# The input projection of the matrix memory in seven quarter products per weight tile

## The reference, cut to what matters

```python
MLSTM_INNER = 2 * D_MODEL       # 2048
def mlstm_mixer(u, w_in, conv_w, conv_b, wq, wk, wv, w_gates, b_gates, norm_w, skip, w_out):
    xm, z = jnp.split(u @ w_in, 2, axis=-1)
    xc = jax.nn.silu(causal_depthwise_conv(xm, conv_w, conv_b))
    q = block_diag_proj(xc, wq)
    k = block_diag_proj(xc, wk)
    v = block_diag_proj(xm, wv)
    ...
    h = (h * norm_w + skip * xc) * jax.nn.silu(z)
    return h @ w_out
```

## Time and profile before

| | us |
|---|---|
| median of three runs | 2719.5 (2718.7 to 2721.1) |
| profiled execution, its own time | 2724.7 |
| its span in the trace | 2722.9 |
| TensorE busy | 2636.3 |
| VectorE / ScalarE / GpSimd busy | 791.6 / 402.8 / 755.3 |

### The profile page before, as it was taken

The page is one execution under the profiler, slowest core; times in us unless marked ns, Lnnn a source line. Parts: engine busy times, 40 slices in busy tenths (PEclk is TensorE's granted clock), DMA queues, the critical chain, the costliest instruction groups (busy, mean ns, idle before and its releaser), DMA issues.

```text
span 2722.9 us, 44432 instructions
## 1 busy us (share of the span) xinstructions
PE 2636.3 (97%) x19521; PEld 1838.0 (68%) x19521; DVE 791.6 (29%) x1463; ACT 402.8 (15%) x813; POOL 755.3 (28%) x585
## 2 busy tenths in 40 slices
PE   7999999989999999999999999999999999999998
PEld 5767888856644444444445436488888878998998
DVE  3316310064300001100013494232221136532651
ACT  0032010020211001000002244110000121221000
POOL 0042055074000000000000260145555331622886
PEclk8999999999999999999999999999999999999999
DMA  9878544468499999999997210332222243122542
GB/s 304 305 256 280 143 158 155 144 250 290 170 353 408 407 373 379 396 390 407 376 387 271 81 47 8 105 105 78 93 85 86 78 139 108 49 76 93 171 162 87
DMA packets 318290, 561.70 MB, mean 206 GB/s; under 512 B 45544, under 2 KB 181520, under 8 KB 317968
## 3 DMA queue, kind: packets, MB, share of 16 engines
q1 hardware_dynamic: 299280, 554.57, 57.2%
q10 hardware_dynamic: 18816, 4.27, 0.8%
HBM read 557.75 MB, written 1.05 MB: 205 GB/s over the span
## 4 chain that ended last, share of the span: by engine, by line
PE 56%; issue 34%; POOL 3%; DVE 2%; POOLq 2%; ACT 1%; DMA 1%; DVEq 1%; SPq 0%; ACTq 0%
PE psum L984 13%; PE psum L1829 10%; PE psum L2058 5%; PE psum L1866 5%; PE psum L1912 3%; PE psum L1150 3%; PE psum L2086 2%; PE psum L1305 2%; PE psum L1932 2%; PE psum L1645 2%; PE psum L1025 1%; PE psum L1959 1%; POOLq L3685 1%; DMA ring<-in_ada_w 1%; POOLq L3583 1%
## 5 line engine op out<-in xcount | busy, mean ns | idle before, releaser
L1507 PE MATMUL psum<-ring,xe 128*32 128x512 f32 (+1 forms) x4608 | 458.0, 557 | 1.6 <-issue 1.4
L1507 PEld LDWEIGHTS psum<-ring,xe 128*32 128x32 f32 x4608 | 152.5, 110 | 294.7 <-issue 255.2
L984 PE MATMUL psum<-act_in,ring 128*128 128x256 f32 x1216 | 269.7, 382 | 2.4 <-DVE act_in L2671 1.3
L984 PEld LDWEIGHTS psum<-act_in,ring 128*128 128x128 f32 x1216 | 231.2, 191 | 42.7 <-issue 9.3
L3684 POOL TENSOR_TENSOR ckv<-ckv,nstat 128x512 f32<-128x512 f32 x2 | 2.5, 1276 | 894.8 <-DVE nstat L3229 894.8
L1529 PE MATMUL psum<-ring,zs 128*32 128x256 f32 x4224 | 232.4, 379 | 0.8 <-DMA ring<-in_moe_w 0.8
L3120 DVE TENSOR_TENSOR act_in<-act_in,psum 128x256 f32<-128x256 f32 (+1 forms) x72 | 28.7, 399 | 630.8 <-ACT act_in L2368 630.8
L1529 PEld LDWEIGHTS psum<-ring,zs 128*32 128x32 f32 x4224 | 137.8, 110 | 97.7 <-issue 7.1
L3697 POOL TENSOR_TENSOR w_sums<-ring 128x512 f32<-128x512 f32 (+1 forms) x34 | 42.3, 1243 | 298.0 <-DVE ctxT L3286 123.8
L2368 ACT ACTIVATE act_in<-psum 128x256 f32<-128x256 f32 (+1 forms) x72 | 26.4, 367 | 573.4 <-PE psum L1507 573.4
L1645 PE MATMUL psum<-a,ring 128*128 128x512 f32 x224 | 97.5, 594 | 2.0 <-ACT a L2417 1.3
(11 more groups left out here) (551 smaller groups left out, 4204.2 us busy)
## 6 DMA issues: line engine op xcount, KB each, us to landing
ring<-in_moe_w SPq DMA_DIRECT2D x216, 1024.0 KB, 11.2
ring<-in_ffn_w SPq DMA_DIRECT2D x97, 1024.0 KB, 5.2
ring<-in_ada_w SPq DMA_DIRECT2D x96, 1024.0 KB, 7.9
ring<-in_moe_w SPq DMA_DIRECT2D x64, 768.0 KB, 6.1
ring<-in_hg_w_in SPq DMA_DIRECT2D x20, 1024.0 KB, 5.1
ring<-in_mlstm_w_in SPq DMA_DIRECT2D x16, 1024.0 KB, 6.2
ring<-in_mlstm_w_out SPq DMA_DIRECT2D x8, 1024.0 KB, 7.4
ring<-in_s_w_glu SPq DMA_DIRECT2D x8, 1024.0 KB, 11.6
```

The costliest lines, as they stand in the source:

```text
L984: last = pe.matmul(bank(j)[:, n * T:(n + 1) * T], tile[:, k * width + n * P:k * width + (n + 1) * P], src(k), start=start and k == 0, stop ...
L1507: last = pe.matmul(psum[rows, r, 0:2 * nb * 32].rearrange("p (u b f) -> p u b f", u=2, b=nb), xe[:, k, at:at + 32], tile[:, :, :, rows], s ...
```

## The change

Each input tile is now computed by one step of Winograd's form of Strassen's method. The 1024 inputs, the 256 outputs of a tile and the 256 tokens are each cut in half. The plain method then is eight products of 512 inputs, 128 outputs and 128 tokens; here there are seven, and additions:

- GpSimd forms four sums of quarters of each weight tile, 128 x 512 each, into `in_w_sums` (two sets, by the parity of the tile). Sum set i waits for the tile's landing and for the last product of tile i - 2. `xT` times the constant moves behind the sums of tile 6, and the work behind the stage waits for the last join, since the buffers lie in `qk`.
- VectorE forms three sums of the activations once (`in_x_sums`, and one in place in `act_in`), between the modulation and the first join.
- TensorE makes seven products (`input_tile`), in the order 1, 2, 6, 5, 7, 3, 4. Product 6 is the first that needs a weight sum (and, for tile 0, the activations' sums). A tile now takes two jobs, the first with products 1, 2 and 6. Of each modulation step the two halves stay behind the tile, but `gate_weights` now stands between the halves.
- ScalarE only copies product 1 out of PSUM (`in_first`); VectorE joins (`join`): five additions, each with one input in PSUM and one in SBUF. The SiLU of `zs` is done in place after the join, one tile later.
- VectorE convolves between the joins, one block per tile up to tile 4, then three per tile, until the 16 blocks are done after tile 8. Gate fold and block diagonals come after joins 9, 10 and 11. ScalarE does the convolution's SiLUs under tiles 8 to 15.

Elsewhere only semaphore counts shift by 16, 8 or 4.

```diff
+INPUT_TILES = 16
...
-JOBS = [("params", 1), ("xT", 4), ("late_params", 4), ("m_in", 8 + EARLY_Z), ("m_fold", 4), ("m_z", 8 - EARLY_Z), ("m_qk", 16), ("m_fsel", 1),
+JOBS = [("params", 1), ("xT", 4), ("late_params", 4), ("m_in", 2 * (8 + EARLY_Z)), ("m_fold", 4), ("m_z", 2 * (8 - EARLY_Z)), ("m_qk", 16), ("m_fsel", 1),
...
+        in_flat = qk.rearrange("p c k t -> p (c k t)")
+        in_w_sums = in_flat[:, 1024:5120].rearrange("p (n i k s) -> p n i k s", n=2, i=4, s=P)
+        in_x_sums = in_flat[:, 5120:6656].rearrange("p (i k t) -> p i k t", i=3, t=P)
+        in_first = in_flat[:, 6656:6912].rearrange("p (n t) -> p n t", n=2)
+        in_with_sixth = in_flat[:, 6912:7040]
+        in_with_two = in_flat[:, 7040:7296].rearrange("p (m t) -> p m t", m=2)
...
+        def in_quarters(i):
+            v = ring[:, in_tile(i) % RING].rearrange("p (e k f s) -> p e k f s", e=2, k=4, f=2)
+            return {(f, e): v[:, e, :, f] for f in range(2) for e in range(2)}
+        def in_product(i, m, n=1):
+            b, at = SMALL_AT[m]
+            return bank(in_job(i) + b)[:, at * P:(at + n) * P]
...
+                def input_tile(i):
+                    wait_tile(pe, in_tile(i))
+                    quarter, sums = in_quarters(i), in_w_sums[:, i % 2]
+                    operands = {1: (quarter[0, 0], lambda k: act_in[:, k, 0:P]),
+                                2: (quarter[0, 1], lambda k: act_in[:, 4 + k, 0:P]),
+                                6: (sums[:, 1], lambda k: in_x_sums[:, 1, k]),
+                                5: (sums[:, 0], lambda k: in_x_sums[:, 0, k]),
+                                7: (sums[:, 2], lambda k: act_in[:, k, P:T]),
+                                3: (sums[:, 3], lambda k: act_in[:, 4 + k, P:T]),
+                                4: (quarter[1, 1], lambda k: in_x_sums[:, 2, k])}
+                    for m, (held, moving) in operands.items():
+                        if m in (1, 5):
+                            wait_free(pe, in_job(i) + SMALL_AT[m][0])
+                        if m == 6:
+                            pe.wait_ge(S("w_sums_ready"), i + 1)
+                        if i == 0 and m in (6, 7, 4):
+                            pe.wait_ge(S("x_sums_ready"), {6: 2, 7: 3, 4: 4}[m])
+                        for k in range(4):
+                            if i == 0 and m in (1, 2):
+                                pe.wait_ge(S("mlstm_in_ready"), (0 if m == 1 else 4) + k + 1)
+                            last = pe.matmul(in_product(i, m), held[:, k], moving(k), start=k == 0, stop=k == 3)
+                            if m == 1 and k == 0:
+                                last.then_inc(tile_begun, 1)
+                        if m in (6, 4):
+                            full(last, in_job(i) + SMALL_AT[m][0])
...
-                    mm_pair(in_tile(j), in_job(j), lambda k: act_in[:, k],
-                            before=(lambda k: pe.wait_ge(S("mlstm_in_ready"), k + 1)) if j == 0 else None)
-                    if FIRST_INPUT - 1 <= j < FIRST_INPUT - 1 + UNDER_INPUT:
-                        ada_step("b", j - FIRST_INPUT + 1, 1)
+                    input_tile(j)
+                    under = FIRST_INPUT - 1 <= j < FIRST_INPUT - 1 + UNDER_INPUT
+                    if under:
+                        ada_half("b", j - FIRST_INPUT + 1, 1, 0)
                     if j == 7 + EARLY_Z:
                         gate_weights()
+                    if under:
+                        ada_half("b", j - FIRST_INPUT + 1, 1, 1)
...
+                def z_silu(i):
+                    wait_out(act, in_job(i) + 1)
+                    act.activation(zs[:, 2 * i - 16:2 * i - 14], zs[:, 2 * i - 16:2 * i - 14], ACT.Silu).then_inc(S("gate_silu_ready"), 1)
                 for i in range(16):
-                    j = in_job(i)
-                    wait_full(act, j)
-                    src = bank(j).rearrange("p (a t) -> p a t", a=2)
-                    if i < 8:
-                        out_of(act.activation(xm[:, 2 * i:2 * i + 2, 4:4 + T], src, ACT.Copy), j)
-                    else:
-                        out_of(act.activation(zs[:, 2 * i - 16:2 * i - 14], src, ACT.Silu), j)
+                    if i >= 2:
+                        wait_out(act, in_job(i - 2) + 1)
+                    wait_full(act, in_job(i))
+                    act.activation(in_first[:, i % 2], in_product(i, 1), ACT.Copy).then_inc(S("first_out"), 1)
+                    if i >= 9:
+                        z_silu(i - 1)
+                    if i >= 8:
+                        for c in (2 * i - 16, 2 * i - 15):
+                            act.wait_ge(S("conv_sum_ready"), c + 1)
+                            act.activation(xc[:, c], xc[:, c], ACT.Silu, bias=col("mlstm_conv_b", c)).then_inc(S("conv_ready"), 1)
+                z_silu(15)
...
-                    act.wait_ge(S("conv_sum_ready"), c + 1)
-                    act.activation(xc[:, c], xc[:, c], ACT.Silu, bias=col("mlstm_conv_b", c)).then_inc(S("conv_ready"), 1)
-                    if c >= 2:
-                        j = job_of["m_qk"] + c - 2
-                        wait_full(act, j)
-                        out_of(act.activation(qk[:, c - 2, 0], bank(j)[:, 0:T], ACT.Copy), j)
-                for c in range(IC - 2, IC):
...
+                x11, x12, x21, x22 = act_in[:, 0:4, 0:P], act_in[:, 0:4, P:T], act_in[:, 4:8, 0:P], act_in[:, 4:8, P:T]
+                dve.drain()
+                dve.tensor_tensor(in_x_sums[:, 0], x12, x11, ALU.subtract).then_inc(S("x_sums_ready"), 1)
+                dve.drain()
+                dve.tensor_tensor(in_x_sums[:, 1], x22, in_x_sums[:, 0], ALU.subtract).then_inc(S("x_sums_ready"), 1)
+                dve.tensor_tensor(x12, x22, x12, ALU.subtract).then_inc(S("x_sums_ready"), 1)
+                dve.drain()
+                dve.tensor_tensor(in_x_sums[:, 2], x21, in_x_sums[:, 1], ALU.subtract).then_inc(S("x_sums_ready"), 1)
+                def join(i):
+                    if i < 8:
+                        flat = xm.rearrange("p c t -> p (c t)")[:, 2 * i * (T + 4):(2 * i + 2) * (T + 4)]
+                        first_at, last_at = flat[:, 4:4 + P], flat[:, T + 8 + P:2 * (T + 4)]
+                        between = flat[:, 4 + P:4 + P + 2 * (P + 4)].rearrange("p (m t) -> p m t", m=2)[:, :, 0:P]
+                    else:
+                        flat = zs[:, 2 * i - 16:2 * i - 14].rearrange("p c t -> p (c t)")
+                        first_at, last_at = flat[:, 0:P], flat[:, 3 * P:4 * P]
+                        between = flat[:, P:3 * P].rearrange("p (m t) -> p m t", m=2)
+                    dve.wait_ge(S("first_out"), i + 1)
+                    dve.tensor_tensor(first_at, in_first[:, i % 2], in_product(i, 2), ALU.add)
+                    out_of(dve.tensor_tensor(in_with_sixth, in_first[:, i % 2], in_product(i, 6), ALU.add), in_job(i))
+                    dve.drain()
+                    wait_full(dve, in_job(i) + 1)
+                    dve.tensor_tensor(in_with_two, in_with_sixth[:, None, :].broadcast_to([P, 2, P]),
+                                      in_product(i, 5, 2).rearrange("p (m t) -> p m t", t=P), ALU.add)
+                    dve.drain()
+                    dve.tensor_tensor(last_at, in_with_two[:, 1], in_product(i, 5), ALU.add)
+                    out_of(dve.tensor_tensor(between, in_with_two, in_product(i, 3, 2).rearrange("p (m t) -> p m t", t=P),
+                                             ALU.add), in_job(i) + 1)
+                    dve.drain()
+                def convolve(c):
...
+                done = 0
+                for i in range(16):
+                    join(i)
+                    for c in range(done, min(done + (1 if i < 5 else 3), IC)):
+                        convolve(c)
+                        done = c + 1
+                    if i == 7 + EARLY_Z:
+                        fold_gates()
+                    elif i == 8 + EARLY_Z:
+                        query_key_rows()
+                        block_diagonals(0, qk_small)
+                    elif i == 9 + EARLY_Z:
+                        block_diagonals(2, qkv_small[:, 2])
...
-            pool.wait_ge(S("mlstm_in_ready"), DC)
-            pool.tensor_scalar(xT[:], xT[:], ALPHA, None, ALU.mult)
+            for i in range(16):
+                wait_tile(pool, in_tile(i))
+                if i >= 2:
+                    wait_full(pool, in_job(i - 2) + 1)
+                quarter, sums = in_quarters(i), in_w_sums[:, i % 2]
+                pool.tensor_tensor(sums[:, 0], quarter[1, 0], quarter[1, 1], ALU.add)
+                pool.tensor_tensor(sums[:, 2], quarter[0, 0], quarter[1, 0], ALU.subtract)
+                pool.drain()
+                pool.tensor_tensor(sums[:, 1], sums[:, 0], quarter[0, 0], ALU.subtract)
+                pool.drain()
+                pool.tensor_tensor(sums[:, 3], quarter[0, 1], sums[:, 1], ALU.subtract).then_inc(S("w_sums_ready"), 1)
+                if i == FIRST_INPUT:
```

(3 more changed lines are left out.)

54 lines of the change are left out of this document (25 added, 29 removed).

## The result

The changed kernel takes 2739.9 us (median of 6 runs, 2735.3 to 2742.7) where the kernel before takes 2719.4 (6 runs): ratio 1.0063, 95% interval 1.0052 to 1.0074. It is slower, by 20.5 us, which is twice the forecast of +9.8 (2729.3) and 1.1 us inside the upper end of its range (2741). A second comparison in a later session (experiment e8_after) gave 2736.4 to 2723.8 us, ratio 1.0046 (1.0033 to 1.0060): +12.6 us. In that session 3 of the 24 runs of the kernel before took 5559 to 7476 us and are left out of its median.

The account below looks back on a forecast made before the run. TensorE, busy 97% of the span, was taken to bound the kernel. The terms -9.9 + 8.3 + 2.0 + 10 + 1.9 - 2.5 gave +9.8 us on the 2719.5 us median: 2729.3 us, range 2713 to 2741.

Parts of the forecast that it names:

- TensorE's own work: Input stage: seven products take 6.25 us a tile instead of 6.91; -9.9 us for fifteen tiles (-7.5 to -11.2).
- The start: Tile 0: GpSimd's sums stretch VectorE's modulations and delay the sixth product; +8.3 us (+0.5 to +11).
- Weight sums behind the load: Middle of the input stage: landing and GpSimd's sums leave TensorE no slack; +2 us over nine tiles (0 to +5).
- Rival D: Input stage: DMA is the bound, no gain in ten tiles between modulation tiles; 2735, chance 0.18 together with Rival C.
- VectorE's backlog at the gates: Gates' products: TensorE waits for late convolutions and joins, +10 us (0 to +18), then lower clock, +1.9 (0 to +4).
- Rival C: Tiles 8 and 9: VectorE's backlog makes TensorE wait there too; about +19 us, 2739, chance 0.18 together with Rival D.
- Behind the stage: Query products: ScalarE, freed of the convolution's SiLUs, no longer paces them; -2.5 us (0 to -3.2).

Follow-up runs that it names:

- e8_after: The changed kernel again, unchanged, timed beside the kernel before in a later session: 2736.4 us, ratio 1.0046.
- e3: Changed kernel without GpSimd's weight sums, TensorE multiplying the loaded quarters instead (values not the reference's): 2712.1 us, ratio 0.9957 to the kernel before.
- e1: Changed kernel with GpSimd beginning its first weight sums only after VectorE's eight modulations: 2735.2 us, ratio 1.0049 to the kernel before.
- e6: Changed kernel with tile 0 by the old 16 products, without sums, GpSimd beginning with tile 1 behind the modulations: 2729.0 us, ratio 1.0022.
- e5: e6 plus e4's edit and one convolution a tile up to tile 12, three behind tile 13: 2712.8 us, ratio 0.9966 to the kernel before.
- e4: Changed kernel with the fourth product moved to third place and TensorE going on after three of four weight sums: 2739.4 us, ratio 1.0056.
- e2: Changed kernel with one channel block's convolution behind each join in all 16 tiles: 2730.8 us, ratio 1.0027 to the kernel before.
- e7: Changed kernel with the gates' products and the fold behind tile 11 instead of tile 9: 2729.6 us, ratio 1.0022 to the kernel before.
- e12: Changed kernel with GpSimd's x times ALPHA moved from behind tile 6's sums to behind tile 15's: 2732.4 us, ratio 1.0039.
- e11: Changed kernel with two convolutions behind each join from the first on: 2738.1 us, ratio 1.0052 to the kernel before.
- e9: Changed kernel with GpSimd's four TENSOR_TENSORs a tile replaced by one-input TENSOR_SCALARs, times one (values not the reference's): 2731.3 us, ratio 1.0028.
- e10: e5 plus the gates' fold ahead of the convolution behind join 9: 2716.0 us, ratio 0.9970 to the kernel before.

## Why the prediction came out right, point by point

**TensorE's own work: right.** 6.25 us a tile; -9.9 us for fifteen tiles, and e3 shows the full 8.30 us with the modulation step too.

**The start: right, by its mechanism.** +8.2 for +8.3: modulations 8.84 us (9 forecast), sixth product at 45.8 (46.4), tile 0 at 52.8 (52.8). e1 takes the overlap away and the modulations are at 0.41 us; e6 takes the sums out of tile 0, and some 3.4 us are left, as waits in tiles 1 to 5 (34.7 us for 31.3); in e5 0.6 are left (31.9).

**Weight sums behind the load: the mechanism right, the term mis-sized.** I gave +2 (0 to +5); it is +6.3: 2.7 in tiles 6 to 9 (35.9 us for 33.2) and 3.6 in tiles 10 to 15 (51.5 us from tile 10's begin to the stage's end, for 47.8). The links of the chain were 1.0 + 5.6 + 5.3 + 0.2 + 4.5 = 16.6 for two tiles; what failed is the 5.6 of the earlier trace rows. In the kernel after the same load takes 7.0 us (median of the issues from 80 to 155 us):

```profile
ring<-in_mlstm_w_in SPq DMA_DIRECT2D x7, 1024.0 KB, 7.0
```

With it the chain is 18.0 us for two tiles, and the profile has 8.31 + 9.77 = 18.1 and 8.43 + 9.37 = 17.8. I had carried a landing time of the kernel before over to this one. The pace is only part of why it grew: e3, at 8.30 us a tile, has 7.4, and in the kernel after the loads behind a short tile took 7.0 and 7.9 us; but those behind a long one (9.77 and 9.37) took 6.4 and 7.6, still more than the 5.4 to 6.1 of before at an even 8.96. What else lengthens them isn't shown. The range, 0 to +5, was too narrow as well. e4, which shortens the chain by 1.8 us, brings 8.48. Rival D gave the right number (no gain in these ten tiles) for a reason that e3 refutes; its own +6 counted the forecast's +2 a second time (ten times 0.66 less 2 is 4.6).

**VectorE's backlog at the gates: right, a little too large.** Wait and clock together +11.9 forecast, +8.8 measured in the first profile (13.3 - 4.5), +10.2 in e8. TensorE stood at the third product 39.7 us after tile 5's end (36 forecast; the chain above had made it late) and went on at 44.9 (47). e2, e7 and e12 each take a part of the backlog or its place away and the wait follows. One link was missing: I had costed GpSimd's x times ALPHA at nothing, and it held one convolution for 3.70 us; e12 prices it at 3 to 4. That VectorE was ready 2 us before my estimate although this link was missing means that I had priced the rest of its work some 5 us too high.

**Rival C: did not occur here, but is real.** TensorE waits in front of no tile before the gates in the changed kernel; in e7 and e11, where the slack runs out elsewhere, it does (1.5 and 7.5 us). Its threshold of 10.5 us in the prediction was wrong: the 8.4 us already hold the 2.05 of the modulation step, to which it adds them again.

**Behind the stage: right.** -2.0 for -2.5. A group of query products takes 2.80 to 2.90 us where the earlier trace rows has 3.17, not the 2.7 that I had reckoned.

**The sum.** -9.9 + 8.2 + 6.3 + 8.8 - 2.0 = 11.4 us by the terms, 11.6 in the profile, 9.8 forecast: two errors of +4.3 and -3.1 that nearly cancel. That the forecast of 9.8 came within 2 us of the stage's 11.6 is in part luck: the weight sums and the backlog were each mis-sized by more. The remaining distance to the measured 20.5 lies outside the stage. In the profile it is 3.4 us, where the clock's level at spots of the later stages differs. In the times, the second comparison gives +12.6, close to the 12.8 of its own profile behind the query products; the first has a median of the kernel before 4.4 us lower (2719.4 for 2723.8; the other sessions have 2722.1 to 2724.1) and one of the changed kernel 3.5 us higher. Why these medians moved between the sessions is not explained, and with it why the measured loss is twice the forecast. The first measurement lies inside the range by 1.1 us only.

## What to carry over

An addition on an idle engine is not free: before work goes to an idle GpSimd, look at what VectorE does at the same microseconds, and price each of its SBUF-to-SBUF instructions there at the length of GpSimd's, where that has two inputs (1.34 us in the median here; beside one-input instructions of 512 columns it was 0.48 to 0.87 in e9). A load's landing time holds for the kernel in which it was read (5.6 us there, 7.0 after the change); where the change puts work behind the landing, take it as a range. And a wait that moves with the schedule (e7, e11, e12) is best removed by giving the late engine its work later, not earlier.

## What the runs showed of the hardware

- VectorE's one-input TENSOR_SCALAR (128x256, SBUF to SBUF) takes 0.41 us alone and 1.35 to 1.48 beside GpSimd's TENSOR_TENSORs of 1.27; beside GpSimd's TENSOR_SCALARs of 1.49 it takes 0.40 to 0.85; of 32 SCALAR_TENSOR_TENSORs beside these 20 took 0.48 us as alone and 12 took 0.67 to 0.87 (e9). By the Trainium skill (SBUF — State Buffer, "Who interferes with whom") an instruction of VectorE's with two SBUF inputs contends with any of GpSimd's that reads SBUF, and the shared pair of ports is an exclusive lock. Beside the TENSOR_TENSORs the traces agree; in e9 GpSimd reads SBUF too, and of the two-input instructions more than half are not held up and none for the length of one of GpSimd's (two of the four sums of x took 0.91 and 1.10 us for 0.69), so there the measurement decides against it.
- But a long TENSOR_SCALAR of GpSimd's (128x2048, 5.4 us) did hold VectorE up, for 3.70 us in the kernel after and in e3 and for 4.89 in e9. Why this one and not those of 512 columns is open.
- TENSOR_TENSORs of VectorE's with one input in PSUM, the joins' additions, kept their 0.28 to 0.42 us beside GpSimd in every profile.
- GpSimd needs 1.49 us for times one on 128x512 (e9) and 1.27 us for an addition of two inputs of that size.
- Two profiles of one kernel had the lower clock near 2200 us at places some 10 us apart; it cost 1.7 us in an unbroken row of products and nothing ahead of a wait.
- TensorE's clock at the start of the input stage differs between executions of nearly the same program: 0.50 up to 40 us in e10, 1.00 from 35 us in e5, 2.7 us in the length of tile 0 (9.72 and 6.98).
